# A two-block transformer layer pair on one core: the modulation weight loaded by columns in quarters, and the low quarters of the output weight on GpSimd

## The chip, the cores and the metric

The kernel runs on one core of a Trainium2 chip. The number that counts is the device time of one execution in microseconds. Before the change it is 2321.15 us, the median of three runs (2320.94 to 2322.6).

A core has five engines that run their own instruction queues strictly in the written order and wait for each other through semaphores: TensorE (PE, matrix products; its weight loads are listed as PEld), VectorE (DVE), ScalarE (ACT), GpSimd (POOL) and SyncE (SP), which here only starts DMA transfers. PE writes into PSUM, eight banks of 512 f32 numbers for each of 128 partitions.

## The reference, cut to what matters

```python
# first block, one layer, S = 1024 tokens, D = 1024
mod   = silu(c) @ w_mod + b_mod            # c: one row; w_mod: 1024 x 6144
mod_c = silu(c_ctx) @ w_mod + b_mod        # the same for the 256 context tokens
sh1, sc1, g1, sh2, sc2, g2 = split(mod, 6)
h  = rms_norm(x, norm1_g) * (1 + sc1) + sh1
hc = rms_norm(ctx, norm1_g) * (1 + csc1) + csh1
q_a, k_a, v_a, q_b, k_b, v_b = in_proj(h, w_in)    # and of hc
# two attentions (a window, a neighbourhood), then
x = x + g1 * (concat(rms_norm(o_a, on_a), rms_norm(o_b, on_b)) @ w_out)
# a gated feed-forward, and a second block with its own mixers and feed-forward
```

All is float32. Nothing can be projected before shift `sh1` and gain `1 + sc1` are known, and these need the first 2048 columns of `w_mod`, 8 MB.

## The kernel before, in words

Large products are made from a value split in two parts that PE multiplies at full rate: a rounded high part (`..._hi`, made by ACT as a copy into the type fp32r) and the rest (`..._lo`, made by DVE as the value less its high part). A product is then three PE instructions: high by high, high by low, low by high. Products that are not split are plain f32; the trace shows each of these as two PE passes.

**The start.** SP issues the loads in the order of the block that begins at line 1634. `mod_w` holds the first 2048 columns of `w_mod`, in eight pieces of 1 MB (rows p·8 + j for partition p, each an 8 KB run), each with a semaphore of its own. Between them stand two tiles of `x` (0.5 MB each) and the first half of the input weight, `stage` (1 MB). Its second half and the other tiles of `x` follow.

PE (block at line 1676) turns the bias rows, then makes the modulation: for each piece j four products (line 1689) of `cond` (128 x 2, the two silu rows) with 512 columns each. The four write to PSUM partitions 0, 32, 64 and 96 of bank 0, so that each uses a column group of PE of its own. Between pieces 2 and 3 it turns the first two token tiles (`pair_turn`, line 392). When all eight are summed, DVE copies the bank (line 1737), PE turns it into columns with four small products (line 1694), and DVE adds the bias and makes `gain_cols` (lines 1741, 1745).

From there the first of four pairs of token tiles is made: `pair_hi` on ACT makes eight slices of 128 columns, gain and shift applied, as high parts (`ht_hi`, line 416), `pair_lo` on DVE the same values unsplit and the low parts (`ht_lo`, lines 425, 431), and `first_pe` multiplies slice by slice with the halves of the input weight (`w_hi`, `w_lo`; lines 521, 522, then 528). The semaphore `chunk_hi` releases one slice at a time. ACT and DVE also split the weight (lines 449, 453). From this pair on PE runs through the projections.

**The attention.** `attention_pe`, `attention_act` and `attention_dve` each walk through 64 units (two phases A and B, four head pairs, eight query blocks) one ahead of the other. Besides, in four units of phase B (`QUARTER_AT`, line 1209) ACT makes a quarter of the high part of the first output weight (`out_hi`, line 1391) and DVE right behind it the quarter of the low part (`out_lo`, line 1400), which needs that high part. GpSimd meanwhile makes the bias tables `edge` and `inner` and scales the rows of phase A (`rows_a`, lines 1451 to 1460).

Of the kernel before, what the change touches and what calls it, by code (L numbers as in the profile page):

```python
# [59 lines left out]
def program(nc, t, out):  # L60
# [40 lines left out]
    nat = region(4 * (NT * D + 2 * 10 * KVW))  # L101
    xnr = region(2 * D * 4)


# [6 lines left out]
    ht_lo = at("ht_lo", [KT, S], F32R, ht + 32768)  # L111
    mod_w = at("mod_w", [8, 2048], F32, ht)
    xn = at("xn", [2, D], F32, xnr)
# [3 lines left out]
    mod_row = at("mod_row", [512], F32, xnr + 6144)  # L117
    mod_part = at("mod_part", [512], F32, xnr)

# [48 lines left out]
    with ctx:  # L168
# [13 lines left out]
        y_made, chunk_hi = early("y_made"), early("chunk_hi")  # L182
        modw_in = [early(f"modw_in{j}") for j in range(8)]
        ctx_landed = early("ctx_landed")
# [223 lines left out]
        def pair_hi(act, i):  # L408
            act.wait_ge(tr_done, 2 * i + 2)
            if i == 0:  # L410
                act.wait_ge(cols_done, 3)
# [90 lines left out]
        def piece_weights(w, part):  # L502
            slot = (P_X + (0, 2, 4, 7)[w] + part) % 2
            return (x[:, slot, :].rearrange("p (k n) -> p k n", k=4) for x in (w_hi, w_lo))

        def first_pe(pe):

            for i in range(4):
# [5 lines left out]
                for part in range(2):  # L514
                    if i == 0:
                        pe.wait_ge(w_lo_done, P_X + part + 1)
# [99 lines left out]
        def act_x(act):  # L616

            sums_of_pair(act, 0)
            split_hi(act, 0, 0)
            pair_hi(act, 0)  # L620
            split_hi(act, 1, 1)
            sums_of_pair(act, 1)
            sums_of_pair(act, 2)
            pair_hi(act, 1)
# [74 lines left out]
        def dve_x(dve):  # L699

            pair_lo(dve, 0)
            split_lo(dve, 1, 1)
            for b in (2, 3):
                root_tile(dve, b, T_X, q_nat[:, b, :])
            pair_lo(dve, 1)
# [153 lines left out]
        def unit(ph, i, n):  # L859
            return 32 * ph + NB * i + n  # L860
# [347 lines left out]

        QUARTER_AT = [unit(B, 2, 3), unit(B, 2, 5), unit(B, 2, 7), unit(B, 3, 0)]

# [70 lines left out]
        def attention_dve(dve):  # L1281
# [3 lines left out]
            for ph, i, n in each_unit():  # L1285
# [39 lines left out]
        def tables_pool(pool):  # L1325
# [67 lines left out]

        def quarter_dve(dve, q):

            if q == 3:
                dve.wait_ge(w_hi_done, P_O + 1)
            else:
                dve.wait_ge(quarter_hi, q + 1)
            low = dve.tensor_tensor(quarter(out_lo0, q), quarter(out_raw, q), quarter(out_hi0, q).bitcast(F32), ALU.subtract)  # L1400
            if q == 3:
                low.then_inc(w_lo_done, 1)
# [11 lines left out]
        def side_dve(dve, q):  # L1414

            if q == 3:
                dve.wait_ge(w_hi_done, P_O + 2)
            else:
                dve.wait_ge(quarter_hi, 3 + q + 1)
# [26 lines left out]

        def rows_a(pool):

# [6 lines left out]
            pool.wait_ge(on_in, 32)  # L1455
            for j in range(NT):
                row = q_nat[:, j, 0:AW]
# [177 lines left out]
        def _(sp):  # L1635
            sp.dma_start(cond[:, 0, :], t["c"][0].rearrange("(p k) -> p k", k=KT)).then_inc(cond_in, 16)
            sp.dma_start(cond[:, 1, :], t["c_ctx"].rearrange("(p k) -> p k", k=KT)).then_inc(cond_in, 16)
            for j in range(8):
                w = t["w_mod"][0].rearrange("(p k) n -> p k n", k=KT)[:, j, 0:2 * D]
                sp.dma_start(mod_w[:, j, :], w).then_inc(modw_in[j], 16)  # L1640
                if j == 0:
                    sp.dma_start(ident[:, :], t["k_ident"]).then_inc(pe_consts_in, 16)
                    sp.dma_start(vec_rows[0:16, :], t["b_mod"][0, 0:2 * D].rearrange("(k n) -> k n", n=P)).then_inc(vec_in, 16)
                    sp.dma_start(vec_rows[16:24, :], t["norm1_g"][0].rearrange("(k n) -> k n", n=P)).then_inc(vec_in, 16)
                if j == 1:
                    for b in range(2):
                        sp.dma_start(q_nat[:, b, :], t["x"][0, b * P:(b + 1) * P, :]).then_inc(x_in[b], 16)
                if j == 4:
                    load_weights(sp, P_X, x_piece(0, 0), in_piece(stage))
            for j in (2, 3):  # L1650
                sp.dma_start(q_nat[:, j, :], t["x"][0, j * P:(j + 1) * P, :]).then_inc(x_in[j], 16)
            load_weights(sp, P_X + 1, x_piece(0, 1))
            for j in range(4, NT):
                sp.dma_start(q_nat[:, j, :], t["x"][0, j * P:(j + 1) * P, :]).then_inc(x_in[j], 16)
# [22 lines left out]
        def _(pe):  # L1677

            pe.wait_ge(pe_consts_in, 16)
            pe.wait_ge(cond_done, 1)  # L1680
            pe.wait_ge(banks_clear, 1)
            pe.wait_ge(vec_in, 32)
            pe.transpose(ps[:, 3, 0:24], vec_rows[0:24, :], ident[0:24, 0:24]).then_inc(vec_turned, 1)
            for j in range(8):
                if j == 3:
                    pair_turn(pe, 0, q_nat[:, 0:2, :])
                pe.wait_ge(modw_in[j], 16)
                for g in range(4):
                    mm = pe.matmul(ps[32 * g:32 * g + 2, 0, :], cond[:, :, j], mod_w[:, j, 512 * g:512 * (g + 1)], start=(j == 0), stop=(j == 7))
            mm.then_inc(part_done, 1)  # L1690
            pe.wait_ge(part_evac, 1)
            rows_of = ident[:, :].rearrange("p (g r) -> p g r", r=32)[:, :, 0:2]
            for e in range(4):
                pe.matmul(ps[:, 2, 8 * e:8 * e + 8], mod_part[:, e * P:(e + 1) * P], rows_of, start=True, stop=True).then_inc(mod_done, 1)

            first_pe(pe)
# [32 lines left out]
        def _(dve):  # L1729
            dve.memset(ps[:, 0, :], 0.0).then_inc(banks_clear, 1)  # L1730
            dve.wait_ge(vec_turned, 1)
            dve.tensor_copy(vec_cols[:, :], ps[:, 3, 0:24]).then_inc(vec_ready, 1)
            for b in range(2):
                root_tile(dve, b, T_X, q_nat[:, b, :])
            split_lo(dve, 0, 0)
            dve.wait_ge(part_done, 1)
            dve.tensor_copy(mod_part[:, :], ps[:, 0, :]).then_inc(part_evac, 1)
            dve.wait_ge(mod_done, 4)
            dve.wait_ge(vec_ready, 1)
            for w in range(2):  # L1740
                dve.tensor_tensor(mod_cols[:, w, :].rearrange("p (g e) -> p g e", e=4),
                                  ps[:, 2, 0:32].rearrange("p (e g w) -> p w g e", g=4, w=2)[:, w],
                                  vec_cols[:, 0:16].rearrange("p (g e) -> p g e", e=4), ALU.add).then_inc(cols_done, 1)
            dve.wait_ge(cols_done, 2)
            dve.scalar_tensor_tensor(out=gain_cols[:, :, :], in0=mod_cols[:, :, KT:16], scalar=1.0, in1=bcast(vec_cols[:, 16:24], 1, 2),
                                     op0=ALU.add, op1=ALU.mult).then_inc(cols_done, 1)
            dve.wait_ge(cols_done, 3)
            dve_x(dve)
# [2146 lines left out]
```

## Time and profile before

| what | value |
|---|---|
| median of three runs | 2321.15 us |
| the profiled execution | 2320.64 us, of which 2318.9 us lie between its first and last instruction |
| PE busy in these | 2263.4 us, 98% |
| DVE, ACT, POOL busy | 1481.0 us (64%), 1020.7 us (44%), 365.6 us (16%) |
| first product of the first token pair | at 35.97 us |
| first product of the second token pair | at 51.12 us |

The profile gives times from the first instruction on. In a timeline a row merges like instructions that follow each other, so its count can be over one. The idle time in square brackets is that of the engine ahead of the row, with what ended it. In a table of stretches PEclk is the clock that TensorE was granted as a share of 2.4 GHz: 1.00 is 2.4 GHz and 0.50 is 1.2 GHz. It is 1.00 as well where the record does not reach yet, before 18.9 us; there the length of PE's passes tells the level.

### The profile page before, as it was taken

The page shows a single profiled execution, that of the slowest core. Times are in us where ns is not written, and L with a number is a line of the kernel's source. Part 1 is how long each engine was busy: PE and PEld are TensorE (multiplying, and loading weights), DVE is VectorE, ACT ScalarE, POOL GpSimd, SP SyncE. Part 2 cuts the span into 40 slices and gives each one's busy share as a digit, 9 for nine tenths or more (in the row PEclk, how much of TensorE's full clock was granted, in tenths as well). Part 3 has the DMA queues.
Part 4 walks back from the last instruction along what each step waited for, and adds up shares of the span by engine and source line. Part 5 has one row for each costly group of instructions (what it writes and reads, how often), then busy time and mean ns, then how long its engine had stood idle before and what let it go on. Part 6 is the DMA issues. An engine that isn't in the chain of part 4 may idle for free. (4 is left out here: it accounts for less than half of the span.)

```text
span 2318.9 us, 34643 instructions
## 1 busy us (share of the span) xinstructions
PE 2263.4 (98%) x12884; PEld 1867.7 (81%) x12884; DVE 1481.0 (64%) x2408; ACT 1020.7 (44%) x2030; POOL 365.6 (16%) x342
## 2 busy tenths in 40 slices
PE   6999999999999999999999999999989999999998
PEld 3878778878878888888888976988878888888886
DVE  3533278776687777776689423234587777666687
ACT  3523178875343232323444433233355555444444
POOL 2493400154340000000001000131240000000011
PEclk9999999999999999999999999999999999999999
DMA  8142350015213232326654411113224444666553
GB/s 321 37 147 90 120 120 28 2 47 167 107 58 124 89 126 86 119 87 214 212 186 142 148 37 46 38 38 143 103 96 150 150 152 148 239 202 217 173 168 123
DMA packets 156129, 289.73 MB, mean 125 GB/s; under 512 B 11998, under 2 KB 59820, under 8 KB 152764
## 3 DMA queue, kind: packets, MB, share of 16 engines
q1 hardware_dynamic: 155964, 287.52, 36.8%
q8 instruction: 104, 1.70, 0.3%
q14 instruction: 61, 0.50, 0.1%
HBM read 219.04 MB, written 70.62 MB: 125 GB/s over the span
## 5 line engine op out<-in xcount | busy, mean ns | idle before, releaser
L2270 PE MATMUL ps<-ff_b_hi,ff_a_hi 128*128 128x512 f32 x448 | 174.5, 390 | 0.2 <-DVE ff_b_lo L2258 0.2
L2271 PE MATMUL ps<-ff_b_lo,ff_a_hi 128*128 128x512 f32 x448 | 174.3, 389 | 0.0
L2272 PE MATMUL ps<-ff_b_hi,ff_a_lo 128*128 128x512 f32 x448 | 174.3, 389 | 0.0
L2231 ACT ACTIVATE ff_a_hi<-ff_a_raw 128x512 fp32r<-128x512 f32 x112 | 70.7, 631 | 157.3 <-PE ps L2272 149.9
L1964 ACT ACTIVATE swiglu_w_hi<-swiglu_stage 128x512 fp32r<-128x512 f32 x110 | 69.0, 630 | 160.6 <-PE ps L2023 151.9
L2021 PE MATMUL ps<-ht_hi,swiglu_w_hi 128*128 128x512 f32 x352 | 137.8, 392 | 0.6 <-DVE ht_lo L1916 0.6
L2022 PE MATMUL ps<-ht_lo,swiglu_w_hi 128*128 128x512 f32 x352 | 137.0, 389 | 0.0
L2023 PE MATMUL ps<-ht_hi,swiglu_w_lo 128*128 128x512 f32 x352 | 137.0, 389 | 0.0
L2256 DVE TENSOR_TENSOR ff_a_lo<-ff_a_raw,ff_a_hi 128x512 fp32r<-128x512 f32 x112 | 80.6, 719 | 83.2 <-ACT ff_a_hi L2231 83.2
L453 DVE TENSOR_TENSOR w_lo<-stage,w_hi 128x2048 fp32r<-128x2048 f32 x23 | 58.9, 2562 | 112.6 <-ACT w_hi L449 112.4
L2270 PE MATMUL ps<-swiglu_b_hi,swiglu_a_hi 128*128 128x512 f32 x308 | 120.3, 391 | 0.4 <-DVE swiglu_b_lo L2258 0.4
L2272 PE MATMUL ps<-swiglu_b_hi,swiglu_a_lo 128*128 128x512 f32 x308 | 119.9, 389 | 0.0
L2271 PE MATMUL ps<-swiglu_b_lo,swiglu_a_hi 128*128 128x512 f32 x308 | 119.9, 389 | 0.0
L328 POOL TENSOR_SCALAR msq<-sumsq 128x1 f32<-128x1 f32 x18 | 7.9, 438 | 674.3 <-ACT junk L340 657.9
L1968 DVE TENSOR_TENSOR swiglu_w_lo<-swiglu_stage,swiglu_w_hi 128x512 fp32r<-128x512 f32 x110 | 77.7, 707 | 46.8 <-ACT swiglu_w_hi L1964 45.0
L2021 PE MATMUL ps<-swiglu_t_hi,swiglu_w_hi 128*128 128x512 f32 x264 | 103.2, 391 | 1.7 <-DVE swiglu_t_lo L1916 1.7
L2023 PE MATMUL ps<-swiglu_t_hi,swiglu_w_lo 128*128 128x512 f32 x264 | 102.8, 389 | 0.0
L2022 PE MATMUL ps<-swiglu_t_lo,swiglu_w_hi 128*128 128x512 f32 x264 | 102.7, 389 | 0.0
L1186 ACT ACTIVATE probs<-masked,small 128x641 f32<-128x641 f32 (+3 forms) x128 | 101.5, 801 | 0.5 <-DVE small L1255 0.5
L2021 PE MATMUL ps<-ht_hi,ff_w_hi 128*128 128x512 f32 x256 | 100.2, 391 | 1.4 <-DVE ht_lo L1916 1.4
L2023 PE MATMUL ps<-ht_hi,ff_w_lo 128*128 128x512 f32 x256 | 99.6, 389 | 0.0
L2022 PE MATMUL ps<-ht_lo,ff_w_hi 128*128 128x512 f32 x256 | 99.6, 389 | 0.0
(466 smaller groups left out, 6479.9 us busy)
## 6 DMA issues: line engine op xcount, KB each, us to landing
ff_a_raw<-ff_act_dram SPq DMA_DIRECT2D x112, 256.0 KB, 2.7
swiglu_a_raw<-swiglu_act_dram SPq DMA_DIRECT2D x77, 256.0 KB, 2.8
stage<-w_in SPq DMA_DIRECT2D x18, 1024.0 KB, 5.2
stage<-w_mod SPq DMA_DIRECT2D x16, 1024.0 KB, 4.6
ff_stage<-w_ff SPq DMA_DIRECT2D x16, 1024.0 KB, 5.4
ff_act_dram<-ff_act_sums SPq DMA_DIRECT2D x16, 1024.0 KB, 4.3
ff_act_dram<-ff_acts SPq DMA_DIRECT2D x16, 768.0 KB, 5.6
swiglu_stage<-w_gate SPq DMA_DIRECT2D x11, 1024.0 KB, 6.3
```

Source lines behind the costliest of these rows:

```text
L453: dve.tensor_tensor(w_lo[:, slot, :], staged(p)[:, :], w_hi[:, slot, :].bitcast(F32), ALU.subtract).then_inc(w_lo_done, 1)
L1186: act.activation(probs_s[:, j, first:8 + CTX + width], masked_s[:, j, first:8 + CTX + width], ACT.Exp, bias=low, scale=-1.0, accum_out=den ...
L1964: act.activation(w7_hi[w_at(q, b)][:, :, :], w_source(q, b), ACT.Copy).then_inc(f.w_hi, 1)
L1968: dve.tensor_tensor(w7_lo[w_at(q, b)][:, :, :], w_source(q, b), w7_hi[w_at(q, b)][:, :, :].bitcast(F32), ALU.subtract).then_inc(f.w_lo, 1)
L2021: pe.matmul(bank(q, b), w7_hi[w_at(q, b)][:, k, :], x_of(0, b, k), start=(k == 0), stop=False)
L2022: pe.matmul(bank(q, b), w7_hi[w_at(q, b)][:, k, :], x_of(1, b, k), start=False, stop=False)
L2023: mm = pe.matmul(bank(q, b), w7_lo[w_at(q, b)][:, k, :], x_of(0, b, k), start=False, stop=(k == 3))
L2231: act.activation(a_hi[r][:, :], a_raw[s % LOOK][:, :], ACT.Copy).then_inc(f.a2_hi, 1)
L2256: dve.tensor_tensor(a_lo[r][:, :], a_raw[s % LOOK][:, :], a_hi[r][:, :].bitcast(F32), ALU.subtract).then_inc(f.a2_lo, 1)
L2270: pe.matmul(bank, a_hi[r][:, cols], b_hi[r][:, :], start=first, stop=False)
L2271: pe.matmul(bank, a_hi[r][:, cols], b_lo[r][:, :], start=False, stop=False)
L2272: return pe.matmul(bank, a_lo[r][:, cols], b_hi[r][:, :], start=False, stop=last)
```

## The change

**The start.** `mod_w` is now laid out as two sides (shift, gain) of eight row groups by 1024 columns and loaded in four quarters: quarter g is columns 256g to 256g + 255 of both sides, by two DMAs of 1 MB in 1 KB runs. The order of the loads is quarter 0, the identity and bias rows, `x` tiles 0 and 1, first weight half, quarter 1, second weight half, quarter 2, `x` tiles 2 and 3, quarter 3, the rest.

`mod_quarter_pe(g)` sums eight products of `cond` with the 512 columns of a quarter, all to partitions 32g of bank 3, waits for DVE's copy, and turns the result into columns with four small products. `mod_quarter_dve(g)` is DVE's share, `quarter_hi_of_pair`, `quarter_y_of_pair` and `half_lo_of_pair` make two slices of the first pair from a quarter. `first_pe` calls quarters 1, 2 and 3 between its products of the first pair.

**The attention.** DVE no longer makes `out_lo`; GpSimd does (`quarter_low`), behind its tables and rows. GpSimd's eight rows are cut into five ahead of the last `inner` and three behind it. The third and fourth quarter on ACT move by one unit.

```diff
+        def mod_quarter_pe(pe, g):
+            pe.wait_ge(modw_in[g], 32)
+            sums = ps[32 * g:32 * g + 2, 3, :].rearrange("p (s n) -> p s n", s=2)
+            for j in range(KT):
+                mm = pe.matmul(sums, cond[:, :, j], mod_w[:, :, j, 256 * g:256 * g + 256], start=(j == 0), stop=(j == KT - 1))
+            mm.then_inc(part_done, 1)
+            pe.wait_ge(part_evac, g + 1)
+            for e in range(4):
+                pe.matmul(ps[:, 2, 8 * e + 2 * g:8 * e + 2 * g + 2], mod_part[:, e * P:(e + 1) * P], ident[:, 32 * g:32 * g + 2],
+                          start=True, stop=True).then_inc(mod_done, 1)
...
+        def quarter_hi_of_pair(act, g):
+            act.wait_ge(tr_done, 2)
+            act.wait_ge(cols_done, 3 * g + 3)
+            for k in (2 * g, 2 * g + 1):
...
         def first_pe(pe):
...
                     for k in range(4):
+                        if i == 0 and k % 2 == 0 and 2 * part + k // 2:
+                            mod_quarter_pe(pe, 2 * part + k // 2)
+                        if i == 0 and k == 0:
+                            pe.wait_ge(w_lo_done, P_X + part + 1)
                         pe.wait_ge(chunk_hi, KT * i + 4 * part + k + 1)
...
-        QUARTER_AT = [unit(B, 2, 3), unit(B, 2, 5), unit(B, 2, 7), unit(B, 3, 0)]
+        QUARTER_AT = [unit(B, 2, 3), unit(B, 2, 5), unit(B, 3, 0), unit(B, 3, 1)]
...
-                if u in QUARTER_AT:
-                    quarter_dve(dve, QUARTER_AT.index(u))
...
                 if i == PAIRS - 1:
-                    rows_a(pool)
+                    roots_a(pool)
+                    rows_a(pool, range(5))
                 for j in range(2):
                     table_inner(pool, i, j)
+            rows_a(pool, range(5, NT))
+            for q in range(4):
+                quarter_low(pool, q)
...
+            def mod_quarter(g):
+                for side in range(2):
+                    first = D * side + 256 * g
+                    sp.dma_start(mod_w[:, side, :, 256 * g:256 * g + 256],
+                                 t["w_mod"][0].rearrange("(p k) n -> p k n", k=KT)[:, :, first:first + 256]).then_inc(modw_in[g], 16)
```

PE at the start, before: `x12` are the four products of three pieces, then come the turned token tiles, the other five pieces, the four small products, and the first pair.

```order
L1683 MATMUL ps<-ident,vec_rows 128x24
L1689 MATMUL ps<-mod_w,cond 2x512 x12
L392 MATMUL ps<-ident,q_nat 128x128 x16
L1689 MATMUL ps<-mod_w,cond 2x512 x20
L1694 MATMUL ps<-ident,mod_part 128x8 x4
L521 MATMUL ps<-w_hi,ht_hi 128x512
```

PE at the same place now:

```order
L1748 MATMUL ps<-ident,vec_rows 128x24
L510 MATMUL ps<-mod_w,cond 2x512 x8
L514 MATMUL ps<-ident,mod_part 128x2 x4
L393 MATMUL ps<-ident,q_nat 128x128 x16
L575 MATMUL ps<-w_hi,ht_hi 128x512
L576 MATMUL ps<-w_lo,ht_hi 128x512
```

and eight products further, where the first two slices of the first pair end:

```order
L576 MATMUL ps<-w_lo,ht_hi 128x512
L510 MATMUL ps<-mod_w,cond 2x512 x8
L514 MATMUL ps<-ident,mod_part 128x2 x4
L575 MATMUL ps<-w_hi,ht_hi 128x512
L576 MATMUL ps<-w_lo,ht_hi 128x512
```

The 32 modulation products are still 32, of 512 columns each; but the first eight now stand ahead of the turned tiles, and the other 24 between products of the first pair.

DVE at the start, before: the two scaled token tiles and the weight's low part stand ahead of the modulation.

```order
L1732 COPY vec_cols<-ps 128x24
L352 TENSOR_SCALAR q_nat<-q_nat,rstd 128x1024 x2
L453 TENSOR_TENSOR w_lo<-stage,w_hi 128x2048
L1737 COPY mod_part<-ps 128x512
L1741 TENSOR_TENSOR mod_cols<-ps,vec_cols 128x16 x2
```

DVE there now, up to the second quarter:

```order
L1788 COPY vec_cols<-ps 128x24
L520 COPY mod_part<-ps 32x512
L525 TENSOR_TENSOR mod_cols<-ps,vec_cols 128x2x2 x2
L529 SCALAR_TENSOR_TENSOR gain_cols<-mod_cols,vec_cols 128x2x2
L353 TENSOR_SCALAR q_nat<-q_nat,rstd 128x1024 x2
L546 TENSOR_SCALAR xn<-ps,gain_cols,mod_cols 128x256 x2
L452 TENSOR_TENSOR w_lo<-stage,w_hi 128x2048
L520 COPY mod_part<-ps 32x512
```

The scaling of the first token tiles and the low part of the first weight half now stand behind the first quarter.

GpSimd near the end of the attention, before: the last scaled row of phase A, the last `inner`, the first row sum of phase B.

```order
L1458 TENSOR_SCALAR q_nat<-q_nat,rstd 128x512
L1460 TENSOR_TENSOR q_nat<-q_nat,on_ab 128x512
L1317 TENSOR_TENSOR inner<-edge_95,col_mask 128x384 x2
L1466 TENSOR_SCALAR msq<-sumsq 128x1
L1468 TENSOR_TENSOR rstd<-msq,neg_half 128x1
```

The same place now:

```order
L1517 TENSOR_SCALAR q_nat<-q_nat,rstd 128x512
L1519 TENSOR_TENSOR q_nat<-q_nat,on_ab 128x512
L1455 TENSOR_TENSOR out_lo_111<-out_raw,out_hi_112 128x512 x4
L1525 TENSOR_SCALAR msq<-sumsq 128x1
L1527 TENSOR_TENSOR rstd<-msq,neg_half 128x1
```

`inner` has moved three rows up, and the four low quarters are GpSimd's last work ahead of the row sums of phase B.

## Rows read from the trace of the kernel before

**Rows 1.** Page, first part: busy time, share of the span, instructions.
```profile
PE 2263.4 (98%) x12884; PEld 1867.7 (81%) x12884; DVE 1481.0 (64%) x2408; ACT 1020.7 (44%) x2030; POOL 365.6 (16%) x342
```

**Rows 2.** Timeline of PE from the start: start, length, line, operation, count, [idle before].
```profile
10.78 1.89 PE L1689 MATMUL ps<-mod_w,cond 128*2 128x512 f32 x8 [1.52 <-DMA mod_w<-w_mod]
15.79 1.89 PE L1689 MATMUL ps<-mod_w,cond 128*2 128x512 f32 x8 [3.12 <-DMA mod_w<-w_mod]
...
20.13 1.90 PE L1689 MATMUL ps<-mod_w,cond 128*2 128x512 f32 x16
...
30.95 1.83 PE L1689 MATMUL ps<-mod_w,cond 128*2 128x512 f32 x8 [0.62 <-DMA mod_w<-w_mod]
33.60 1.06 PE L1694 MATMUL ps<-ident,mod_part 128*128 128x8 f32 x8 [0.82 <-DVE mod_part L1737]
35.97 0.73 PE L521 MATMUL ps<-w_hi,ht_hi 128*128 128x512 f32 x1 [1.30 <-ACT ht_hi L416]
...
47.55 1.91 PE L392 MATMUL ps<-ident,q_nat 128*128 128x128 f32 x16
49.21 2.07 PE L528 MATMUL ps<-w_hi,ht_lo 128*128 128x512 f32 x8
51.12 0.39 PE L521 MATMUL ps<-w_hi,ht_hi 128*128 128x512 f32 x1
```

**Rows 3.** Table of stretches, three head pairs of phase B: us, busy of each engine, PEclk.
```profile
447.00:476.20 29.20, 29.15 (x343) 24.60 (x342) 21.89 (x61) 24.89 (x67) 4.05 (x4) 1.00 0.01 3
476.20:507.80 31.60, 29.16 (x343) 24.62 (x342) 22.64 (x63) 24.41 (x63) 26.08 (x20) 1.00 0.33 84
507.80:537.70 29.90, 28.39 (x330) 24.07 (x330) 19.77 (x55) 25.25 (x67) 14.03 (x16) 1.00 0.01 2
```

**Rows 4.** DMA issues of the page: times, KB each, median us to landing.
```profile
stage<-w_mod SPq DMA_DIRECT2D x16, 1024.0 KB, 4.6
...
swiglu_stage<-w_up SPq DMA_DIRECT2D x11, 1024.0 KB, 5.2
```

**Rows 5.** PE's instructions by line and form, whole span: one group.
```profile
L3009 PE MATMUL ps<-zv,ws_t 128*128 128x512 f32 x16 | 7.2, 592 | 0.0
```

**Rows 6.** Timeline of DVE from the start, and one row of ACT.
```profile
15.60 0.75 DVE L352 TENSOR_SCALAR q_nat<-q_nat,rstd 128x1024 f32<-128x1024 f32 x1 [0.73 <-POOL rstd L332]
25.39 2.29 DVE L453 TENSOR_TENSOR w_lo<-stage,w_hi 128x2048 fp32r<-128x2048 f32 x1 [9.04 <-ACT w_hi L449]
...
35.20 3.92 DVE L425 TENSOR_SCALAR xn<-ps,gain_cols,mod_cols 128x256 f32<-128x256 f32 x8
39.16 2.36 DVE L431 TENSOR_TENSOR ht_lo<-xn,ht_hi 128x1024 fp32r<-128x1024 f32 x2
...
35.26 3.81 ACT L416 ACTIVATE ht_hi<-ps,mod_cols,gain_cols 128x256 fp32r<-128x256 f32 x8 [9.90 <-DVE gain_cols L1745]
```

**Rows 7.** Stretches at the start: us, busy of PE, PEld, DVE, ACT, POOL, then PEclk.
```profile
25.80:32.50 6.70, 5.33 (x24) 0.33 (x24) 1.88 (x1) 0.00 (x0) 0.00 (x0) 0.50 1.01 407
32.70:35.90 3.20, 1.14 (x12) 0.97 (x8) 1.82 (x6) 0.64 (x2) 0.00 (x0) 1.00 1.05 403
36.10:39.30 3.20, 3.20 (x8) 2.52 (x9) 3.04 (x8) 3.20 (x8) 0.00 (x0) 0.50 1.03 408
```

**Rows 8.** Waits of 300 us to 600 us: total us, times, longest us.
```profile
PE ps L1086 <- DVE small L1255: 4.5, 5, 1.4
...
DVE out_lo L1400 <- ACT out_hi L1391: 5.2, 4, 1.7
```

**Rows 9.** GpSimd by line and form (470 us to 525 us), and one timeline row.
```profile
L1460 POOL TENSOR_TENSOR q_nat<-q_nat,on_ab 128x512 f32<-128x512 f32 x8 | 10.2, 1279 | 0.7
...
522.35 0.19 POOL L1466 TENSOR_SCALAR msq<-sumsq 128x1 f32<-128x1 f32 x1 [16.30 <-ACT junk L1435]
```

More of the change, by code:

```diff
@@ L111, in program @@
     ht_lo = at("ht_lo", [KT, S], F32R, ht + 32768)
-    mod_w = at("mod_w", [8, 2048], F32, ht)
+    mod_w = at("mod_w", [2, KT, S], F32, ht)
     xn = at("xn", [2, D], F32, xnr)
@@ L182, in program @@
         y_made, chunk_hi = early("y_made"), early("chunk_hi")
-        modw_in = [early(f"modw_in{j}") for j in range(8)]
+        modw_in = [early(f"modw_in{j}") for j in range(4)]
         ctx_landed = early("ctx_landed")
@@ new lines, in mod_quarter_dve @@
+        def mod_quarter_dve(dve, g):
+            dve.wait_ge(part_done, g + 1)
+            dve.tensor_copy(mod_part[32 * g:32 * g + 32, :], ps[32 * g:32 * g + 32, 3, :]).then_inc(part_evac, 1)
+            dve.wait_ge(mod_done, 4 * g + 4)
+            if g == 0:
+                dve.wait_ge(vec_ready, 1)
+            for w in range(2):
+                dve.tensor_tensor(mod_cols[:, w, :].rearrange("p (s k) -> p s k", s=2)[:, :, 2 * g:2 * g + 2],
+                                  ps[:, 2, 0:32].rearrange("p (s h g w) -> p w g s h", s=2, h=2, w=2)[:, w, g],
+                                  vec_cols[:, 0:16].rearrange("p (s k) -> p s k", s=2)[:, :, 2 * g:2 * g + 2], ALU.add).then_inc(cols_done, 1)
+            dve.wait_ge(cols_done, 3 * g + 2)
+            dve.scalar_tensor_tensor(out=gain_cols[:, :, 2 * g:2 * g + 2], in0=mod_cols[:, :, KT + 2 * g:KT + 2 * g + 2], scalar=1.0,
+                                     in1=bcast(vec_cols[:, 16 + 2 * g:18 + 2 * g], 1, 2), op0=ALU.add, op1=ALU.mult).then_inc(cols_done, 1)
@@ new lines, in quarter_hi_of_pair, with quarter_y_of_pair @@
+        def quarter_hi_of_pair(act, g):
+            act.wait_ge(tr_done, 2)
+            act.wait_ge(cols_done, 3 * g + 3)
+            for k in (2 * g, 2 * g + 1):
+                source, gain, shift = pair_source(0, k)
+                act.activation(pair_tokens(0, 0)[:, k, :], source, ACT.Identity, bias=shift, scale=gain).then_inc(chunk_hi, 1)
+        def quarter_y_of_pair(dve, g):
+            dve.wait_ge(cols_done, 3 * g + 3)
+            dve.wait_ge(chunk_hi, 2 * g + 2)
+            for k in (2 * g, 2 * g + 1):
+                source, gain, shift = pair_source(0, k)
+                made = dve.tensor_scalar(pair_y(0)[:, k, :], source, gain, shift, ALU.mult, ALU.add)
+            if g % 2:
+                made.then_inc(y_made, 1)
@@ L506, in first_pe, with half_lo_of_pair @@
+        def half_lo_of_pair(dve, half):
+            ks = slice(4 * half, 4 * half + 4)
+            dve.wait_ge(y_made, half + 1)
+            dve.wait_ge(chunk_hi, 4 * half + 4)
+            dve.tensor_tensor(pair_tokens(0, 1)[:, ks, :], pair_y(0)[:, ks, :], pair_tokens(0, 0)[:, ks, :].bitcast(F32),
+                              ALU.subtract).then_inc(tl_done, 1)
         def first_pe(pe):
@@ L619, in act_x @@
             split_hi(act, 0, 0)
-            pair_hi(act, 0)
+            quarter_hi_of_pair(act, 0)
+            quarter_hi_of_pair(act, 1)
             split_hi(act, 1, 1)
+            quarter_hi_of_pair(act, 2)
             sums_of_pair(act, 1)
+            quarter_hi_of_pair(act, 3)
             sums_of_pair(act, 2)
@@ L699, in dve_x @@
         def dve_x(dve):
[L701 to L704, printed above, removed]
             pair_lo(dve, 1)
@@ L1392, in quarter_act, with quarter_low @@
             done_hi.then_inc(w_hi_done if q == 3 else quarter_hi, 1)
-        def quarter_dve(dve, q):
+        def quarter_low(pool, q):
             if q == 3:
-                dve.wait_ge(w_hi_done, P_O + 1)
+                pool.wait_ge(w_hi_done, P_O + 1)
             else:
-                dve.wait_ge(quarter_hi, q + 1)
-            low = dve.tensor_tensor(quarter(out_lo0, q), quarter(out_raw, q), quarter(out_hi0, q).bitcast(F32), ALU.subtract)
+                pool.wait_ge(quarter_hi, q + 1)
+            low = pool.tensor_tensor(quarter(out_lo0, q), quarter(out_raw, q), quarter(out_hi0, q).bitcast(F32), ALU.subtract)
             if q == 3:
@@ L1455, in rows_a @@
             pool.wait_ge(on_in, 32)
-            for j in range(NT):
+        def rows_a(pool, tiles):
+            for j in tiles:
                 row = q_nat[:, j, 0:AW]
@@ L1637, in _, with x_rows @@
             sp.dma_start(cond[:, 1, :], t["c_ctx"].rearrange("(p k) -> p k", k=KT)).then_inc(cond_in, 16)
[L1638 to L1651, printed above, removed]
+            def mod_quarter(g):
[3 more added lines that the diff above has]
+                                 t["w_mod"][0].rearrange("(p k) n -> p k n", k=KT)[:, :, first:first + 256]).then_inc(modw_in[g], 16)
+            def x_rows(first):
+                for j in (first, first + 1):
+                    sp.dma_start(q_nat[:, j, :], t["x"][0, j * P:(j + 1) * P, :]).then_inc(x_in[j], 16)
+            mod_quarter(0)
+            sp.dma_start(ident[:, :], t["k_ident"]).then_inc(pe_consts_in, 16)
+            sp.dma_start(vec_rows[0:16, :], t["b_mod"][0, 0:2 * D].rearrange("(k n) -> k n", n=P)).then_inc(vec_in, 16)
+            sp.dma_start(vec_rows[16:24, :], t["norm1_g"][0].rearrange("(k n) -> k n", n=P)).then_inc(vec_in, 16)
+            x_rows(0)
+            load_weights(sp, P_X, x_piece(0, 0), in_piece(stage))
+            mod_quarter(1)
             load_weights(sp, P_X + 1, x_piece(0, 1))
+            mod_quarter(2)
+            x_rows(2)
+            mod_quarter(3)
             for j in range(4, NT):
@@ L1680, in _ @@
             pe.wait_ge(cond_done, 1)
-            pe.wait_ge(banks_clear, 1)
+            pe.wait_ge(banks_clear, 2)
             pe.wait_ge(vec_in, 32)
[L1683 to L1694, printed above, removed]
+            pe.transpose(ps[:, 2, 32:56], vec_rows[0:24, :], ident[0:24, 0:24]).then_inc(vec_turned, 1)
+            mod_quarter_pe(pe, 0)
+            pair_turn(pe, 0, q_nat[:, 0:2, :])
             first_pe(pe)
@@ L1729, in _ @@
         def _(dve):
-            dve.memset(ps[:, 0, :], 0.0).then_inc(banks_clear, 1)
+            dve.memset(ps[:, 3, :], 0.0).then_inc(banks_clear, 1)
+            dve.memset(mod_part[:, :], 0.0).then_inc(banks_clear, 1)
             dve.wait_ge(vec_turned, 1)
-            dve.tensor_copy(vec_cols[:, :], ps[:, 3, 0:24]).then_inc(vec_ready, 1)
+            dve.tensor_copy(vec_cols[:, :], ps[:, 2, 32:56]).then_inc(vec_ready, 1)
+            dve.wait_ge(banks_clear, 2)
+            mod_quarter_dve(dve, 0)
             for b in range(2):
                 root_tile(dve, b, T_X, q_nat[:, b, :])
+            quarter_y_of_pair(dve, 0)
             split_lo(dve, 0, 0)
[L1736 to L1747, printed above, removed]
+            mod_quarter_dve(dve, 1)
+            quarter_y_of_pair(dve, 1)
+            half_lo_of_pair(dve, 0)
+            split_lo(dve, 1, 1)
+            mod_quarter_dve(dve, 2)
+            quarter_y_of_pair(dve, 2)
+            for b in (2, 3):
+                root_tile(dve, b, T_X, q_nat[:, b, :])
+            mod_quarter_dve(dve, 3)
+            quarter_y_of_pair(dve, 3)
+            half_lo_of_pair(dve, 1)
             dve_x(dve)
```

10 lines of the change are left out of this document (4 added, 6 removed).

## The prediction, made before the changed kernel ran

> **What bounds the kernel now.** I read the page's busy times first. PE works 2263.4 us of the span [rows 1], so the end is set by PE's work and by the stretches in which it has none. The change touches two of these: the start, and phase B of the attention.
>
> The start is read from PE's timeline [rows 2]. Until 35.97 us PE multiplies modulation pieces as they land, with idle time released by the DMA of `mod_w`. The first pair's products begin at 35.97 us and the second pair's at 51.12 us; from there PE runs on. A change of the start is therefore worth what it does to the moment at which the second pair begins, 51.1 us. Note the row at 20.13 us: sixteen passes (eight products of 512 f32 columns) took 1.90 us, since four column groups work at the same time.
>
> In phase B, three head pairs with like work are compared [rows 3]. In the first, 447.0 to 476.2 us, PE is busy 29.15 of 29.2 us. The next two hold the four quarters of the first output weight, and PE is idle 2.4 of 31.6 and 1.5 of 29.9 us.
>
> **The loads.** Pieces of 1 MB land at an even rate. The row at 15.79 us waited for the fourth MB of the queue, the one at 30.95 us for the tenth [rows 2]: 2.53 us each, the n-th at 5.7 + 2.53n. Runs of 1 KB instead of 8 KB cost more: a lone 1 MB load took 5.2 us to land in 1 KB runs (`w_up`) and 4.6 us in 8 KB runs (`w_mod`) [rows 4]. I add 0.6 us for each MB of quarters and keep 0 as the other end. Quarters 0 to 3 end at the 2nd, 6th, 9th and 12th MB, so they land at 12.0, 23.3, 32.1 and 40.9 us (without the 0.6: 10.8, 20.9, 28.5, 36.1). The Trainium skill, "DMA: Bandwidth & Descriptors", Specifications, puts the smallest transfer for line rate at 512 B, by which the 0.6 us would be nothing and quarter 0 and the whole sum 1.2 us earlier. The two load rows speak against that rule.
>
> **A quarter's products.** Eight products are again sixteen passes of 512 columns, but all write to the same 32 partitions, so no pass has a neighbour group to run beside. No row of the start shows this. The nearest is the group of sixteen plain f32 passes of 512 columns that use the whole array one after the other: 7.2 us [rows 5], as against 1.90 us at 20.13 us. I take 7.2 us, with 1.9 us as the other end (that is a rival below). The four quarters together are 28.8 us of PE where the 32 products cost 7.6 us at the same clock level, and most of those 7.6 us lay in time that PE waited for loads anyway.
>
> **The way from a quarter to its slices.** Before, the last modulation product ended at 30.95 + 1.83 = 32.78 us; copy, four small products and DVE's additions followed, ACT's first slice began at 35.26 us [rows 6] and PE's product at 35.97 us: 2.5 + 0.7 = 3.2 us in which PE does 1.06 us of work. Every quarter has this way once, on PE's path, since PE stands in `mod_quarter_pe` for the copy and then for `chunk_hi`.
>
> Step by step, at the high clock:
> - Quarter 0: 12.0, products to 19.2, columns ready 21.7. Behind them on DVE now stand two scaled token tiles (2 x 0.75, to 23.2). PE turns the second tile (half of the 1.66 us between the rows at 47.55 and 49.21 us, to 24.1). ACT makes two slices (3.81 / 8 each, to 25.1), DVE its two (3.92 / 8 each, to 26.1) and only then the low weight half, 2.29 us, to 28.4 [rows 2, 6]. PE's first product waits for this. Eight products take 1.91 us (49.21 to 51.12), to 30.3.
> - Quarter 1 landed at 23.3, so it waits for nobody: 30.3 + 7.2 + 3.2 + 1.9 = 42.6. The low products wait for DVE: columns 40.0, ACT's slices 41.0, DVE's 42.0, half of the 2.36 us of `ht_lo` 43.2; then 1.9, to 45.1.
> - Quarter 2: 45.1 + 12.3 = 57.4. Quarter 3: 57.4 + 12.3 = 69.7. Then the turned tiles 1.7 and the low products 1.9: 73.3.
>
> The second pair begins at 73.3 instead of 51.1 us: +22.2 us. Loads no longer matter (quarter 3 lands 16 us before PE asks for it), and ACT, POOL and SP have time: their work for the second pair is that of before and lies beside these quarters. What is late next is PE alone, so nothing gives the 22 us back.
>
> **The clock.** PE does not start at 2.4 GHz: 6.7 us from 25.8 us, after an idle wait, ran at 1.2 GHz, and so did 36.1 to 39.3 us, behind the 3.2 us way from modulation to slices in which PE was busy 1.14 us [rows 7]. A low stretch of 3.2 us costs half of it, 1.6 us. I count one at quarter 0, one after the 4.3 us wait for the low weight half (24.1 to 28.4), and, of the three later ways of 3.2 us, half: 1.6 + 1.6 + 2.4 = 5.6 us (ends: 0, and 1.6 + 3.3 + 4.8 = 9.7). The second pair then begins at 78.9, +27.8 us; ends +22.2 and +31.9, and 1.2 us less with the loads' other end.
>
> **The low quarters on GpSimd.** DVE waited 5.2 us in all for `out_hi` of ACT before its four `out_lo`, longest 1.7 us, with the scores' minimum of the next unit queued behind; PE waited 4.5 us for that minimum [rows 8]. Of PE's idle time, 2.4 + 1.5 = 3.9 us in the two head pairs [rows 3] is all that can come back. DVE's share goes; ACT's quarter stays, and ACT is busy 24.4 of 31.6 us there [rows 3]. I take -3.2 us (ends -0.5 and -3.9). GpSimd pays 4 x 1.28 us, the price of a 128x512 product there, and has 16.3 us of idle time ahead of its row sums [rows 9], so this costs nothing; `inner` comes earlier. Should GpSimd be late, the first output product at the attention's end would wait.
>
> **Sum.** +27.8 - 3.2 = +24.6 us. The profiled execution, 2320.64 us, becomes 2345.2; the median of before lies 0.5 us higher, so 2346 us. The forecast's own range: +22.2 - 1.2 - 3.9 = +17.1 to +31.9 - 0.5 = +31.4, that is 2338 to 2353 us.
>
> **Rivals.**
> - *Not slower: a quarter's passes overlap after all.* If sixteen passes of one group cost 1.9 us as the four groups did, each quarter saves 5.3 us. Then loads bind: quarter 3 lands at 40.9 and the pair ends at 40.9 + 1.9 + 3.2 + 1.9 + 3.6 = 51.5, or 46.7 with the loads' other end: +0.4 to -4.4, less 3.2 us. That gives 2314 to 2318 us, about no change or a little faster. For it: only the four-group rows exist at this place. Against: at 20.13 us each group's own next pass came only a quarter of 1.90 us later. The point from which it decides is a quarter's products of about 1.7 us, since 4 x 5.5 us is the loss. 10%.
> - *The clock stays low through the quarters*, because one column group in place of four is little work. Then each quarter costs 14.4 us, and the slices' products, small products and waits between, some 7 us in all, double: +22.2 + 28.8 + 7 = +58, less 3.2: 2376 us. For it: the stretch from 25.8 us stayed at 0.50 though PE was busy 5.33 of 6.7 us. Against: at 32.7 us the clock was at 1.00 after nothing but such products. 12%. The Trainium skill, "TensorE: Matmul & The Clock Gate", Part 1, has activity release a throttle that is the default; no run here shows whether a single group's passes count for it.
> - *GpSimd's part brings nothing*, since ACT's high quarter holds the unit up: 2349 us, within the forecast's own range.
>
> **How the numbers follow.** Forecast with the last rival 78%, low clock 12%, overlap 10% (8 of it no change, 2 faster). A measurement here can tell about 0.2%, 4.6 us, from no change. Slower 0.90, same 0.08, faster 0.02. The range takes the forecast's own, 1 us below it, and reaches up into the cases between it and the low clock: 2337 to 2362 us.
>
> **What would show it.** In the changed profile a quarter's sixteen passes should take near 7 us (near 2 us if the overlap rival holds, 14 us if the low clock does), PE's waits for the DMA of `mod_w` should be left for quarter 0 alone, the first product should follow `w_lo` at about 28 to 31 us, and the second pair begin at 73 to 83 us. In phase B the waits of PE for the minimum should fall from 4.5 us to under 1.5 us. The prediction is wrong if the second pair begins before 60 us.

## The result

The change makes the kernel slower, by 1.2%: 2350.55 us (median of four runs, 2348.49 to 2356.24) against 2321.64 us (four runs), ratio 1.012 with a 95% interval of 1.0106 to 1.0133. In the profiled executions the span went from 2318.9 to 2349.0 us, +30.1 us. The forecast was 2346 us, range 2337 to 2362.

PE's timeline of the changed kernel answers [rows 2]: start, length, line, operation, count, and in brackets the idle time ahead of the row. L510 are a quarter's products, L514 its small products, L575 the first product with slices of that quarter.

```profile
12.31 0.27 PE L1748 MATMUL ps<-ident,vec_rows 24*128 24x24 f32 x1 [12.31 <-DMA vec_rows<-norm_g]
12.51 8.40 PE L510 MATMUL ps<-mod_w,cond 128*2 128x512 f32 x16
21.76 1.05 PE L514 MATMUL ps<-ident,mod_part 128*128 128x2 f32 x8 [0.85 <-DVE mod_part L520]
23.99 1.97 PE L393 MATMUL ps<-ident,q_nat 128*128 128x128 f32 x16 [1.19 <-DVE q_nat L353]
30.38 0.80 PE L575 MATMUL ps<-w_hi,ht_hi 128*128 128x512 f32 x1 [4.42 <-DVE w_lo L452]
...
34.09 7.85 PE L510 MATMUL ps<-mod_w,cond 128*2 128x512 f32 x16
42.72 1.05 PE L514 MATMUL ps<-ident,mod_part 128*128 128x2 f32 x8 [0.78 <-DVE mod_part L520]
44.96 0.50 PE L575 MATMUL ps<-w_hi,ht_hi 128*128 128x512 f32 x1 [1.18 <-ACT ht_hi L538]
...
50.58 7.03 PE L510 MATMUL ps<-mod_w,cond 128*2 128x512 f32 x16
58.39 1.05 PE L514 MATMUL ps<-ident,mod_part 128*128 128x2 f32 x8 [0.78 <-DVE mod_part L520]
60.72 0.77 PE L575 MATMUL ps<-w_hi,ht_hi 128*128 128x512 f32 x1 [1.27 <-ACT ht_hi L538]
...
64.40 8.06 PE L510 MATMUL ps<-mod_w,cond 128*2 128x512 f32 x16
73.25 1.05 PE L514 MATMUL ps<-ident,mod_part 128*128 128x2 f32 x8 [0.79 <-DVE mod_part L520]
75.48 0.50 PE L575 MATMUL ps<-w_hi,ht_hi 128*128 128x512 f32 x1 [1.18 <-ACT ht_hi L538]
...
82.64 0.39 PE L575 MATMUL ps<-w_hi,ht_hi 128*128 128x512 f32 x1
```

Sixteen passes take 7.03 to 8.40 us where before they took 1.90 us. The idle times come in the same pattern with every quarter, about 0.8 and 1.2 us, and once 4.42 us for the low weight half. No row of PE waits for `mod_w` any more. The second pair begins at 82.64 us instead of 51.12 us: +31.5 us.

Stretches of the same time answer [rows 7]: us, busy of PE, PEld, DVE, ACT, POOL, then PEclk.

```profile
29.00:35.80 6.80, 5.42 (x11) 2.74 (x12) 1.33 (x1) 0.00 (x0) 0.00 (x0) 0.50 1.07 371
35.90:46.00 10.10, 8.14 (x28) 2.86 (x26) 1.61 (x6) 1.66 (x3) 0.00 (x0) 1.00 1.05 395
46.10:49.40 3.30, 3.30 (x9) 2.18 (x8) 3.27 (x3) 1.06 (x1) 0.00 (x0) 0.50 0.57 196
49.50:59.60 10.10, 9.16 (x29) 2.83 (x28) 1.23 (x4) 0.00 (x0) 0.00 (x0) 1.00 0.56 205
59.80:66.40 6.60, 5.68 (x11) 2.83 (x12) 2.62 (x5) 3.21 (x6) 1.71 (x4) 0.50 0.00 0
66.60:76.60 10.00, 8.03 (x27) 2.93 (x26) 1.70 (x6) 1.74 (x3) 0.00 (x0) 1.00 0.00 0
76.80:80.10 3.30, 3.30 (x14) 2.90 (x13) 1.44 (x2) 1.28 (x4) 2.84 (x5) 0.50 0.00 0
```

Four times the clock is at 1.2 GHz: the first time it falls within the 4.42 us wait, the third time within the second idle time of quarter 2, the other two times 1.1 and 1.3 us behind a quarter's second idle time. In these stretches PE is busy 5.42 + 3.30 + 5.68 + 3.30 = 17.7 us; half of this, 8.9 us, is my estimate of the price.

The last two of the three head pairs of [rows 3] have lost their idle time (29.10 and 28.50 us, before 31.60 and 29.90), and of the wait for the minimum of [rows 8] there is left, in 300 to 600 us, 1.6 us once. That one lies at the attention's start and is not new: before has it too, ahead of 300 us. In phase B none is left.

```profile
508.80:537.90 29.10, 29.05 (x341) 24.57 (x340) 21.88 (x60) 24.30 (x63) 23.20 (x18) 1.00 0.34 92
537.90:566.40 28.50, 28.35 (x331) 24.07 (x331) 18.91 (x53) 25.10 (x68) 22.05 (x23) 1.00 0.01 2
```
```profile
PE ps L1139 <- DVE small L1308: 1.6, 1, 1.6
```

Matched instruction by instruction from the end, PE's work of after lies behind that of before by 31.5 us from the second pair on, 32.6 us at the head pairs, 28.6 us behind them, and 30.1 us at the end. So the start costs 31.5 us and phase B gives back 4.0. The steps of +1.1 and +1.5 us are mostly stretches at 1.2 GHz elsewhere, in code that the change doesn't touch (below).

### The profile page after: what moved, and what is told of

It reads as the page before. It is cut to its first block and busy times, and to the rows that moved or that the text cites. A ratio compares the mean times of both kernels' runs of the same rounds, so it can differ in the third digit from the quotient of the medians.

```text
span 2349.0 us, 34713 instructions
## 1 busy us (share of the span) xinstructions
PE 2292.2 (98%) x12908; PEld 1879.7 (80%) x12908; DVE 1482.7 (63%) x2417; ACT 1022.5 (44%) x2030; POOL 367.9 (16%) x346
```

## The experiments

All times are medians. A time of before is from the same chip as the run: 2322.05 us, unless another is given. The ratios have intervals of 95%; they differ by up to 0.13% from the quotients of the medians. Every kernel has one profile, and its total is that of one execution, so gains are read from the shift of PE's instructions at the place and from the medians.

**One part alone.** Edit: the second part of the change alone (GpSimd's low quarters and the moved units), then the first part alone.

> The kernel before with the second part of the change alone: GpSimd makes the low quarters of the first output weight, and the third and fourth high quarter move by one unit on ACT; the start is that of before. Theory (DVE stood in front of the low quarters, and PE behind DVE): all of PE's idle time in the two head pairs of phase B, 3.9 us, comes back, as the shift between the traces of before and after fell there from +32.6 to +28.6 us; about 2317.5 us, PE's waits for the minimum below 1.5 us in the whole attention. The prediction's own number for this part was -3.2 us, 2318.4. Rival (ACT's high quarter holds the unit up, and the gain seen between the traces belongs to the shifted start): 2321 to 2322 us, and PE waits for the minimum as before.

Measured: 2318.12 us, before 2322.05; ratio 0.9987, interval 0.9978 to 0.9995. PE's work lies 0.1 us ahead of before at the three head pairs' begin and 4.0 us ahead behind them, and 4.2 us at the end. Phase B has no wait for the minimum left, so the rival (2321 to 2322 us) falls.

> The change's first part alone: modulation weight in quarters at the start, with the low quarters of the output weight left to DVE as before. Theory (the two parts add up): second pair begins at 82 to 83 us as in the changed kernel, the time is 31 to 32 us above before, 2352 to 2355 us, and the waits for the minimum are again 4 to 6 us. Rival (the parts are not independent: the later start shifts ACT's and DVE's work against the loads and GpSimd): under 2350 or over 2357 us.

Measured: 2354.07 us, ratio 1.0137 (1.0124 to 1.0151), as the theory had it. The second pair begins at 84.0 us, and the waits are back (the longest of the five is that of the attention's start, the other four, 3.7 us, are phase B's):

```profile
84.00 0.39 PE L575 MATMUL ps<-w_hi,ht_hi 128*128 128x512 f32 x1
```
```profile
PE ps L1139 <- DVE small L1308: 5.3, 5, 1.6
```
```profile
511.90:543.30 31.40, 29.11 (x342) 24.56 (x342) 22.46 (x63) 24.38 (x63) 26.40 (x20) 1.00 0.31 85
```

The two parts add up: the start alone loses 32.0 us, the quarters on GpSimd alone gain 3.9, and both together are at +28.9. The first part is the whole loss. Its start is that of the changed kernel, and the clock falls in the same four places, but the second pair begins 1.4 us later: so much can lie between two profiles of the same start.

**DVE or ACT in the way?** The second part has two edits, the moved units and the low quarters on GpSimd (with its rows cut in five and three), so each was made alone on the kernel before.

```diff
-        QUARTER_AT = [unit(B, 2, 3), unit(B, 2, 5), unit(B, 2, 7), unit(B, 3, 0)]
+        QUARTER_AT = [unit(B, 2, 3), unit(B, 2, 5), unit(B, 3, 0), unit(B, 3, 1)]
```

> The kernel before with one edit: the third and fourth quarter of the first output weight move by one unit, on ACT and DVE alike; DVE keeps the low quarters. Theory (the low quarters on DVE are the cost, not the units): PE's waits for the minimum stay at 4 to 6 us and phase B is within 0.7 us of before. Rival (ACT's place is the cost): phase B gains 1.5 to 4 us.

Measured: 2324.12 us, ratio 1.0001 (0.9989 to 1.0012). The head pairs take 31.5 and 29.7 us; phase B gains 0.4 us, and four waits for the minimum, 4.1 us, stay between 300 and 600 us.

> The kernel before with the low quarters on GpSimd, but the high quarters of ACT in their old units. Theory (DVE was in the way): phase B gains 3.3 to 4 us as with both edits. Rival (ACT's high quarter in its old unit holds PE up): phase B gains under 2 us.

Measured: 2317.47 us, ratio 0.9973 (0.9962 to 0.9984). The stretches of this kernel:

```profile
477.40:506.50 29.10, 29.05 (x341) 24.57 (x340) 21.87 (x60) 24.25 (x63) 23.22 (x18) 1.00 0.31 91
506.50:535.00 28.50, 28.35 (x331) 24.07 (x331) 18.89 (x53) 25.16 (x68) 21.98 (x23) 1.00 0.01 2
```

All 4.0 us come back without the moved units. ACT is as busy as before, 24.25 against 24.41 us [rows 3]; of the work of DVE and ACT there only DVE's share of the quarters is gone. The rival in which ACT's high quarter holds the unit up falls.

**Are the passes serial because they share a column group?** The eight products of a quarter go to four groups in turn, and the small products add the four rows up:

```diff
-            sums = ps[32 * g:32 * g + 2, 3, :].rearrange("p (s n) -> p s n", s=2)
             for j in range(KT):
+                sums = ps[32 * (j % 4):32 * (j % 4) + 2, 3, :].rearrange("p (s n) -> p s n", s=2)
...
-                pe.matmul(..., mod_part[:, e * P:(e + 1) * P], ident[:, 32 * g:32 * g + 2],
+                pe.matmul(..., mod_part[:, e * P:(e + 1) * P], group_sum[:, :],
```

> The changed kernel, but the eight products of a quarter go in turn to four column groups (partitions 0, 32, 64, 96 of the bank), two to each, and the small products add the four rows up. Theory (sixteen passes of one group run one after the other, 7.0 to 8.4 us; beside each other they take about 1.9 to 2.1 us): a quarter's products fall to about 2 us, PE waits again for the loads of quarters 1 to 3, the second pair begins at 52 to 60 us and the time falls to 2320 to 2328 us. Rival (the ways from quarter to slices and the clock's falls are the larger share): the quarters get short but the second pair begins only at 62 to 70 us, 2330 to 2338 us. Rival (a quarter's passes are bound by something other than the group, such as reading the 512 columns): 7 us each as before and 2350 us.

Measured: 2331.87 us, ratio 1.0046 (1.0031 to 1.006). PE's timeline of this kernel:

```profile
31.20 2.85 PE L511 MATMUL ps<-mod_w,cond 128*2 128x512 f32 x16
34.87 1.05 PE L517 MATMUL ps<-group_sum,mod_part 128*128 128x2 f32 x8 [0.82 <-DVE mod_part L523]
37.10 0.79 PE L578 MATMUL ps<-w_hi,ht_hi 128*128 128x512 f32 x1 [1.18 <-ACT ht_hi L541]
...
42.32 1.90 PE L511 MATMUL ps<-mod_w,cond 128*2 128x512 f32 x16
...
50.70 1.90 PE L511 MATMUL ps<-mod_w,cond 128*2 128x512 f32 x16
...
62.82 0.39 PE L578 MATMUL ps<-w_hi,ht_hi 128*128 128x512 f32 x1
```

The cause is shown: the same sixteen passes take 1.90 us at the high clock over four groups and 7.03 us in one, 3.7 times as much. The Trainium skill, "TensorEngine Tiling (Array Packing)", When to Use Tiling, gives 4× column tiling for a left operand with a free dimension of 32 (`cond` has 2); the trace agrees with 3.7, with the four groups as the condition. But my size was a miss, and the first rival's held: the second pair begins at 62.8 us, not at 52 to 60, and PE still never waits for a later quarter's load. With short passes 19.8 us of the 31.5 are gone. The other 11.7 us are the ways from quarter to slices, the wait for the low weight half among them, and the clock.

**The ways.** One kernel lets PE multiply quarter g + 1 before the slices of quarter g (the passes stay in one group):

```diff
-                            mod_quarter_pe(pe, 2 * part + k // 2)
+                            mod_turn_pe(pe, 2 * part + k // 2)
+                            if 2 * part + k // 2 < 3:
+                                mod_quarter_pe(pe, 2 * part + k // 2 + 1)
```

> The changed kernel, but PE multiplies quarter g + 1 before the slices of quarter g, so that the copy, the additions and the slices of ACT and DVE lie beside PE's products; the passes stay in one group. Theory (each way of 3.2 us was idle time of PE and brought the clock down behind it): the three later ways but the last vanish, no stretch at half clock is left between 36 and 75 us, quarters of 6.9 to 7.2 us each, the second pair begins at about 65 us and the time is 2331 to 2336 us. Rival (the clock falls for another reason, so little work in one column group being enough): the falls stay, and only the ways' own idle time of some 6.6 us is saved, 2344 us.

Measured: 2340.23 us, ratio 1.0073 (1.0058 to 1.0088). The second pair begins at 67.5 us, 15.2 us earlier than in the changed kernel, and behind 30.6 us no stretch at the start is at half clock, though the passes are still in one group. So the rival, by which the clock still falls, is out:

```profile
67.46 0.39 PE L580 MATMUL ps<-w_hi,ht_hi 128*128 128x512 f32 x1
```
```profile
30.70:75.00 44.30, 43.12 (x167) 23.36 (x166) 22.09 (x36) 16.64 (x30) 10.10 (x12) 1.00 0.54 197
```

The time misses the 2331 to 2336 us expected: of the 15.2 us only 10.7 arrive (18.2 us over before, against 28.9). In the profiled execution PE's work lies 16.4 us behind before at 250 us and 21.9 us at the end, although phase B gained 4.0 us on the way: behind that place its record has six stretches at 1.2 GHz between 300 and 1500 us, where the code is that of the changed kernel, which has three there.

**The wait for the low weight half.** The changed kernel with DVE's order changed:

```diff
+            for b in range(2):
+                root_tile(dve, b, T_X, q_nat[:, b, :])
+            split_lo(dve, 0, 0)
             mod_quarter_dve(dve, 0)
-            for b in range(2):
-                root_tile(dve, b, T_X, q_nat[:, b, :])
             quarter_y_of_pair(dve, 0)
-            split_lo(dve, 0, 0)
```

> The changed kernel with one edit in DVE's order: the two scaled token tiles and the low weight half stand ahead of quarter 0's copy and columns, in place of behind them. Theory (PE's 4.4 us wait for the low weight half is paid in full and brings a stretch at 0.50 with it): the copy comes about 0.8 us later, but tiles and weight are ready when the columns are; the first product of the first pair moves from 30.4 to about 26 us, the second pair from 82.6 to 75 to 79 us, and the time is 2343 to 2347 us. Rival (the wait is filled by the next one, as quarter 1 or its slices are late for their own reasons): the first product moves but the second pair stays within 2 us of 82.6, 2349 to 2351 us.

Measured: 2341.46 us, before 2323.45; ratio 1.0082 (1.0061 to 1.0104). Rows of PE's timeline:

```profile
26.21 0.47 PE L575 MATMUL ps<-w_hi,ht_hi 128*128 128x512 f32 x1 [0.75 <-ACT ht_hi L538]
...
28.22 7.03 PE L510 MATMUL ps<-mod_w,cond 128*2 128x512 f32 x16
...
74.02 0.39 PE L575 MATMUL ps<-w_hi,ht_hi 128*128 128x512 f32 x1
```

The first product comes 4.2 us earlier, the second pair 8.6 us earlier, more than expected: the wait costs its own length and about as much again, since quarter 1 now runs in 7.03 us and only 6.8 us at the start are at 1.2 GHz, in place of 20.5. The way of quarter 1 is as long as before (idle times of 0.77 and 1.18 us), but no fall follows it here; behind those of quarters 2 and 3 the clock falls for 3.4 us each.

**Is it idle time that brings the clock down?** The changed kernel with sixty extra products at the start, whose results nobody reads: four before each turn of a quarter, eight behind each turn of quarters 1 to 3, and twenty before the first slices:

```diff
+        def filler(pe, g, n):
+            spare = 32 * ((g + 1) % 4)
+            for _ in range(4 * n):
+                pe.matmul(ps[spare:spare + 2, 3, 0:P], cond[:, :, 0], ident[:, :], start=True, stop=True)
```

> The changed kernel with extra plain products of 2 x 128 columns on PE, into PSUM rows that are written anew later, in the places where PE otherwise stands still at the start: about 0.9 us before each turn of a quarter, 1.8 us after it, 3.5 us before the first slices. They compute nothing that is used. Theory (idle time brings the clock down some microseconds later): the four stretches at 0.50 between 28 and 81 us, 20.5 us together, vanish or shrink to one, and although the extra products overshoot the waits by up to 0.6 us each, the second pair begins at 74 to 79 us in place of 82.6 and the time is 2341 to 2347 us. Rival (the level falls because a single column group is too little work, idle time or not): the stretches stay, and the second pair begins at 83 to 86 us, 2351 to 2354 us.

Measured: 2344.02 us, ratio 1.0082 (1.0063 to 1.0101). Below stand the second pair's first product, one row of stretches that covers the whole start, and the same stretch of the changed kernel:

```profile
75.99 0.39 PE L583 MATMUL ps<-w_hi,ht_hi 128*128 128x512 f32 x1
```
```profile
28.00:81.00 53.00, 49.71 (x243) 27.30 (x241) 21.09 (x35) 14.56 (x26) 9.73 (x10) 1.00 0.50 183
```
```profile
28.00:81.00 53.00, 44.64 (x129) 20.59 (x130) 14.75 (x25) 9.26 (x15) 5.45 (x9) 0.81 0.51 182
```

All four stretches are gone and the second pair begins at 76.0 us, 6.7 us earlier, though PE does more work. The rival, by which the stretches stay, falls. Not all waits were filled: the sixteen products before the turns ran beside the quarters (see the last section), and PE still waited 0.8 us for DVE's copy in every quarter. So the group of extra products behind the turns and that in the 4.4 us wait were enough here. That idle time and not the single column group lowers the clock at the start rests on this run and on the one with the ways, which has no extra products and keeps every quarter in one group. The Trainium skill, "TensorE: Matmul & The Clock Gate", Part 1, has activity release a throttle that is the default; here both levels and this direction agree (0.81 without, 1.00 with the extra products).

**All repairs together.** Four groups, the next quarter ahead of the slices, the weight half ahead of DVE's slices, quarter 3 loaded ahead of the second two token tiles, and DVE's share of it ahead of their scaling.

> The quarters over four column groups, PE's next quarter ahead of the slices of the last one, the low weight half ahead of DVE's share of the first two slices, quarter 3 loaded ahead of the token tiles 2 and 3, and the low quarters on GpSimd. Theory (passes in one group, ways on PE's path and the clock behind them were the three losses; without them the loads bind): PE waits for the loads of quarters 1 to 3 again, quarter 3 lands at about 38.3 us, and the second pair begins at 38.3 + 1.9 + 3.2 + 1.9 + 1.7 + 2.0 = 49 us, at most 54 us; with the 4 us of phase B the time is 2315 to 2321 us, about that of the kernel with GpSimd's part alone (2318). Rival (something of the quartered start is still slow that the two separate runs did not show): second pair after 56 us and 2324 us or more.

Measured: 2319.82 us, before 2322.05; ratio 0.9987 (0.9977 to 0.9996). PE waits for loads again, those of quarters 1 and 2; quarter 3 had landed at 38.4 us, before PE came to it at 39.0:

```profile
23.82 3.59 PE L511 MATMUL ps<-mod_w,cond 128*2 128x512 f32 x16 [1.34 <-DMA mod_w<-w_mod]
...
32.56 1.90 PE L511 MATMUL ps<-mod_w,cond 128*2 128x512 f32 x16 [2.32 <-DMA mod_w<-w_mod]
...
50.48 0.39 PE L583 MATMUL ps<-w_hi,ht_hi 128*128 128x512 f32 x1
```

The second pair begins at 50.5 us, 0.6 us earlier than before the change, which is less than the 1.4 us that lay between two profiles of one start. So with these repairs the whole loss is gone; the order of the loads was not tried by itself. But the quartered start is then worth next to nothing: its kernel is no faster than the one with GpSimd's part alone (2319.82 against 2318.12 us). Three kernels here beat the kernel before, by 0.13 to 0.27% in the ratios, and with it the changed one; the intervals of the three overlap, and the simplest of them is the kernel before with the low quarters on GpSimd and its rows cut in five and three.

## Why the prediction held, and where not

**Loads: right.** Quarters 0 to 3 landed at 11.8, 23.4, 32.2 and 40.7 us by the trace's landing records; the forecast had 12.0, 23.3, 32.1 and 40.9. The two halves of a quarter land 3.0 us apart (37.7 and 40.7), the pieces of before 2.5 us (15.7, 18.2, 20.7). So runs of 1 KB did cost more, 0.5 us per MB against the 0.6 forecast, and the rule of the Trainium skill, "DMA: Bandwidth & Descriptors", Specifications, by which runs of 512 B would do, did not hold here. As said, it did not matter, since PE came late to three of the quarters.

**A quarter's products: right.** 7.03 us at the high clock against 7.2; the overlap rival is out, and the run over four groups shows why it would have needed them.

**The chain at the high clock: right but for the clock.** The three later ways took 3.0 to 3.1 us (the second: passes' end 34.09 + 7.85 = 41.94, first product 44.96) against 3.2. The first product came at 30.4 against 28.4 us, with DVE's low weight half last, as forecast: 0.5 us of it since PE's first product waited to 12.31 us for the bias rows, which are queued behind quarter 0 and had no term, and 1.2 us since quarter 0's passes took 8.40 us. Low clock through the quarters, the second rival, did not come.

**The clock: the term that was too small.** I counted 5.6 us (ends 0 and 9.7): a full fall for quarter 0 and one for the 4.4 us wait, and half of one for each of the other three ways. Up to the second pair it was 10.3 us, above the upper end: 1.4 us in quarter 0's own passes (8.40 against 7.03), which begin before the record of the clock does, and 8.9 us in the four stretches. The wait brought one of 6.8 us, where I had counted 3.2, and each of the later ways had its own, one of them 6.8 us long, where I had counted half of one each. Products and ways were 1.1 us shorter than counted (4 x 0.17 and 3 x 0.15), the beginning 0.5 us later: 78.9 + 4.7 - 1.1 + 0.5 = 83.0, against 82.6 us in the row.

**GpSimd's quarters: right, and a little better.** -4.0 us against -3.2: all idle time of the two head pairs came back, just past the upper end of 3.9. My reason for taking less, that ACT's share stays, was wrong: ACT had time. GpSimd made them in 1.28 us each, as priced.

**The sum.** Forecast +27.8 - 3.2 = +24.6; the profiled executions +31.5 - 4.0 + 2.6 = +30.1, the medians +28.9. The 2.6 us (1.1 ahead of phase B's head pairs, 1.5 behind them) come mostly from the clock's low stretches elsewhere and had no term at all. Before had two of them behind the start, 3.4 us each; after has one of 3.4 us at 329 us, one of 6.8 us at 678 us (3.4 us before), a new one at 1490 us, and none where before had one at 1623 us.

**What stays open** is what decides these later stretches. Most follow idle time of PE at fixed places of the program, as here in the changed kernel ahead of 329 us,

```profile
325.80:329.20 3.40, 1.20 (x16) 0.87 (x14) 2.98 (x7) 3.37 (x6) 0.00 (x0) 1.00 0.81 274
329.40:332.60 3.20, 3.20 (x20) 2.76 (x19) 1.78 (x4) 1.17 (x3) 0.00 (x0) 0.50 0.85 328
```

but the one at 1490 us follows none. There PE is busy without a break, ahead of it for 3.63 us with 32 passes of two columns each:

```profile
1485.34 3.63 PE L3097 MATMUL ps<-mix_c,la 128*128 128x2 f32 x32
...
1490.00:1493.20 3.20, 3.20 (x17) 3.20 (x16) 0.00 (x0) 0.00 (x0) 0.00 (x0) 0.50 0.79 275
```

So idle time accounts, by the runs above, for the stretches at the start, but not for all in this program. And the same place has such a stretch in one run and none in another: the kernel with only the units moved has three between 670 and 1470 us that before lacks, and ends 5.8 us behind it in the profile although its median differs by 2.1 us and its ratio is 1.0001. No run was made to tell it.

## What to carry to other kernels

Before small products are cut into pieces that can start earlier, see whether the pieces still fill the column groups side by side: the cut along columns kept the count of products and made them 3.7 times as long. A piece also brings its own way through copy, turn and slices; put the next piece's products ahead of it, or PE pays the way once per piece, and, as in most of the ways here, a second time in clock. A step that an engine does for later use, as DVE did the low parts here, is best moved to the engine that has idle time there, since the cost lies not in its own duration (0.7 us a quarter here) but in what is queued behind it.

## What the runs showed of the hardware

- Products for another column group were taken up ahead of their turn and ran beside those of the first; the section on the chip says that every engine keeps strictly to the written order, and for PE that is too strong. In the kernel with the extra products, these (L522) stand behind the quarter's products (L510), but the first of them ran before the quarter ended at 20.70 us (the same in all four quarters):

```profile
12.32 7.09 PE L510 MATMUL ps<-mod_w,cond 128*2 128x512 f32 x13
18.83 0.60 PE L522 MATMUL ps<-ident,cond 128*2 128x128 f32 x4
...
19.68 1.02 PE L510 MATMUL ps<-mod_w,cond 128*2 128x512 f32 x2
```

- At this start idle time of PE was paid about twice: a wait of 4.4 us cost 8.6 us in the second pair's begin, and sixty extra products that nobody reads took 6.7 us off it.
- Executions of one kernel lie several microseconds apart: the eight of the kernel before with GpSimd's low quarters alone went from 2315.77 to 2325.09 us. The profiled one is the slowest of them, with five stretches of 3.4 or 6.8 us at 1.2 GHz behind the start where before has two. A smaller difference is read from the shift of PE's instructions at the place, not from the total.
